# Hyena convolution in a diffusion backbone: spectra at odd half-bins, filters computed ahead of two norm gaps, u transformed from even and odd times apart

## The reference, cut to what matters

```python
def hyena_mixer(h, w_in, short_w, ..., bias, w_out):          # h: (1, 256, 1024)
    x0, x1, v = jnp.split(short_conv(h @ w_in, short_w), 3, axis=-1)
    h_fwd, h_bwd = hyena_filters(n, w1, b1, w2, b2, w3, b3, w4, freq)
    u = v * x1
    return (x0 * (bidirectional_long_conv(u, h_fwd, h_bwd) + u * bias)) @ w_out

def bidirectional_long_conv(u, h_fwd, h_bwd):                 # n = 256
    k = concatenate([h_fwd, zeros(1), h_bwd[1:][::-1]])       # 512 taps
    y = irfft(rfft(u, 512) * rfft(k, 512), 512)[:n]
```

## Time and profile before

| | |
|---|---|
| median of three runs | 1348.87 us |
| profiled execution, its own time | 1346.94 us |
| span of its trace | 1345.3 us |
| TensorE matmul busy | 1312.9 us, 98% |
| VectorE busy | 978.9 us, 73% |
| ScalarE busy | 633.8 us, 47% |
| POOL busy | 119.0 us, 9% |
| moved by DMA | 275.13 MB, mean 205 GB/s |
| mean granted TensorE clock | 0.999 |

### The profile page before, as it was taken

How to read it: one execution, slowest core, us unless ns; L and a number is a source line. 1 busy time by engine, 2 the same in 40 slices (tenths; PEclk the granted TensorE clock), 3 DMA queues, 4 the chain that set the end, 5 groups by cost and what they waited for, 6 DMA issues and landing times.

```text
span 1345.3 us, 21575 instructions
## 1 busy us (share of the span) xinstructions
PE 1312.9 (98%) x7850; PEld 1126.2 (84%) x7850; DVE 978.9 (73%) x1446; ACT 633.8 (47%) x969; POOL 119.0 (9%) x209
## 2 busy tenths in 40 slices
PE   5899999999999999999999999999999999999997
PEld 3678777887778988789999999999877888989996
DVE  5888777887776875668888578877765787865554
ACT  6633333323465575565444465444454434644443
POOL 3000010111000430011111001100000000000000
PEclk9999999999999999999999999999999999999999
DMA  9655666777656753269888649875533435656663
GB/s 357 215 173 189 215 215 223 239 256 263 214 159 190 190 155 89 94 214 353 309 301 287 184 156 328 310 220 178 161 116 110 138 112 192 237 183 184 184 184 105
DMA packets 76360, 275.13 MB, mean 205 GB/s; under 512 B 9226, under 2 KB 9781, under 8 KB 75712
## 3 DMA queue, kind: packets, MB, share of 16 engines
q1 hardware_dynamic: 52128, 187.00, 43.1%
q0 software_dynamic: 24160, 87.12, 19.3%
HBM read 273.04 MB, written 1.05 MB: 204 GB/s over the span
## 4 chain that ended last, share of the span: by engine, by line
PE 88%; DVE 5%; ACT 3%; DMA 2%; issue 1%; DVEq 0%; SPq 0%; ACTq 0%
PE gu L1670 17%; PE gu L1672 17%; PE gu L1671 17%; PE acc L1731 8%; PE acc L1733 8%; PE acc L1732 8%; PE acc L1720 1%; DMA wlo<-in_wstream_dram 1%; DVE wlo_r L1002 1%; PE acc L2140 1%; ACT whi L616 1%; PE acc L2016 1%; DVE wlo_r L1327 1%; PE acc L2027 1%; DMA x_lat<-in_x_in_dram 1%
## 5 line engine op out<-in xcount | busy, mean ns | idle before, releaser
L1670 PE MATMUL gu<-h_hi,whi 128*128 128x256 f32 (+1 forms) x1688 | 520.0, 308 | 3.6 <-DVE h_lo L1127 1.3
L1671 PE MATMUL gu<-h_lo,whi 128*128 128x256 f32 (+1 forms) x1688 | 514.6, 305 | 0.0
L1672 PE MATMUL gu<-h_hi,wlo_r 128*128 128x256 f32 (+1 forms) x1688 | 514.3, 305 | 0.0
L1002 DVE TENSOR_TENSOR wlo_r<-wlo,whi 128x1024 fp32r<-128x1024 f32 x350 | 421.6, 1222 | 95.9 <-ACT whi L616 94.2
L616 ACT ACTIVATE whi<-wlo 128x1024 fp32r<-128x1024 f32 x350 | 360.7, 1049 | 92.1 <-DMA wlo<-in_wstream_dram 91.6
L1670 PEld LDWEIGHTS gu<-h_hi,whi 128*128 128x128 f32 x1688 | 318.0, 188 | 31.9 <-issue 3.8
L1671 PEld LDWEIGHTS gu<-h_lo,whi 128*128 128x128 f32 x1688 | 318.1, 188 | 20.5 <-issue 2.1
L1672 PEld LDWEIGHTS gu<-h_hi,wlo_r 128*128 128x128 f32 x1688 | 318.6, 189 | 15.5
L1019 DVE SCALAR_TENSOR_TENSOR part<-wm,cvec,part 128x512 f32<-128x512 f32 x266 | 199.3, 749 | 6.8 <-DMA wm<-in_wmod_dram 0.2
L1731 PE MATMUL acc<-whi,act_hi 128*128 128x512 f32 x440 | 175.8, 400 | 1.7 <-DVE act_lo L1215 1.2
L1733 PE MATMUL acc<-wlo_r,act_hi 128*128 128x512 f32 x440 | 174.2, 396 | 0.0
(11 more groups left out here) (340 smaller groups left out, 1241.7 us busy)
## 6 DMA issues: line engine op xcount, KB each, us to landing
wlo<-in_wstream_dram SPq DMA_DIRECT2D x350, 512.0 KB, 3.7
wm<-in_wmod_dram POOLq DMA_DIRECT2D x132, 512.0 KB, 5.9
...
x_lat<-in_x_in_dram SPq DMA_DIRECT2D x1, 1024.0 KB, 7.8
area<-in_ctx_in_dram SPq DMA_DIRECT2D x1, 1024.0 KB, 8.8
```

The costliest lines, as they stand in the source:

```text
L1002: nc.vector.tensor_tensor(wlo[:, u.base % RING, :], raw[:, u.base % RING, :], whi[:, u.base % RING, :].bitcast(F32), ALU.subtract).then_in ...
L1670: nc.tensor.matmul(out_, w_hi, x_hi, start=start, stop=False, skip_group_check=True)
L1671: nc.tensor.matmul(out_, w_hi, x_lo, start=False, stop=False, skip_group_check=True)
L1672: return nc.tensor.matmul(out_, w_lo, x_hi, start=False, stop=stop, skip_group_check=True)
```

## The change

The transform's bins move from k to k + 1/2 (k = 0 to 255 of 512). No bin is then purely real, so the Nyquist spectra, their copies, the 1x512 product step and the zeroing of a row of `k_s` go: eight spectra in place of ten. The second block of 128 bins is stored in reverse order (255 down to 128), so that row k of it is bin 255-k.

Positions in time are stored even ones first, then odd ones: in the positional features, the window, the tables, and in u, whose transposes now take every second column (`th::2`). Between bins k and 255-k the cosine sums of the even times are equal and their sine sums have opposite signs; for the odd times it is the other way round. So `u_spectrum` makes one matmul per bank and not two (bank 0 even cosine, 1 odd sine, 2 odd cosine, 3 even sine), ScalarE copies banks 2 and 3 to SBUF (`odd_out`, one 1024-wide step for each half, ODD_AT), and VectorE adds them to and subtracts them from banks 0 and 1 (steps 0 and 1) into `u_f`, which lies in SBUF in the spare unit buffers. The four products then read `u_f` and no longer `acc`. A half has eight steps on VectorE, all 1024 wide.

The filters are computed in ffn(1), turns 8 to 10, with steps two units apart. Spectra 0 to 3 (first half of the channels) stand in the gap ahead of ffn(2), three ahead of the norm columns and one behind them, and the 16 warm-up matmuls of that gap are gone; spectra 4 to 7 stand in the same way in the gap ahead of the hyena stage. ScalarE copies two of each four between the steps of its norms and two behind `h_his` (`spectra_norms`). `filter_out(i)` waits only until VectorE has read the banks of the one before (FD_READ), not for its whole sums. The hyena units carry no spectra. The eight inverse transforms stay where they are.

The diff, cut to its core and less indented; new table values for the time order and half-bins stand at its end.

```diff
@@ -218,8 +218,8 @@
 def sem(name):
...
-spare_hi = sb("spare_hi", [P, UNIT], F32R)
-spare_lo = sb("spare_lo", [P, UNIT], F32R)
+spare, spare_r = both("spare", [P, 2, UNIT])
+spare_hi, spare_lo = spare_r[:, 0, :], spare_r[:, 1, :]
@@ -322,6 +321,7 @@
+u_f = spare[:, :, :].rearrange("p w (s n) -> p w s n", s=2)
@@ -388,7 +388,7 @@
 def spectrum_bank(i):
-    return [gu[:, 0, :], gu[:, 1, :], job_p[:, :]][i] if i < 3 else [mean_p[:, :], job_p[:, :]][(i - 3) % 2]
+    return four_banks[i % 4]
 def scores(i):
@@ -923,11 +924,6 @@
-    ffn(1, peeled=at_steps([(6, 2)], [lambda: batch_rows(1)]))
-    load_table(ACT.Sqrt)
-    norms(8, (U_FFN[2] + 2, U_FFN[2] + 3))
-    load_table(ACT.Silu)
     def sine(l):
@@ -937,24 +933,29 @@
-        if what == "nyquist":
-            ins = nc.scalar.activation(k_nyq[half][0:1, :], spectrum_bank(i)[0:1, :], ACT.Copy)
-        else:
-            ins = nc.scalar.activation((k_re if what == "re" else k_s)[:, w, cols], spectrum_bank(i), ACT.Copy)
-        ins.then_inc(fa, 1)
-    ffn(2, peeled=at_steps([ROWS_AT] + FILTER_AT, [lambda: batch_rows(2)] + [lambda l=l: sine(l) for l in range(3)]))
+        nc.scalar.activation((k_re if what == "re" else k_s)[:, w, cols], spectrum_bank(i), ACT.Copy).then_inc(fa, 1)
+    def spectra_norms(q, held, i):
+        square(q, 0)
+        square(q, 1)
+        split(Unit(held))
+        square(q + 1, 0)
+        spectrum_out(i)
+        square(q + 1, 1)
+        spectrum_out(i + 1)
+        split(Unit(held + 1))
+        h_his(q + 1)
+        spectrum_out(i + 2)
+        spectrum_out(i + 3)
+    ffn(1, peeled=at_steps([(6, 2)] + FILTER_AT, [lambda: batch_rows(1)] + [lambda l=l: sine(l) for l in range(3)]))
...
-    square(10, 0)
-    square(10, 1)
-    split(Unit(U_HY + 2))
-    spectrum_out(0)
-    square(11, 0)
-    square(11, 1)
-    spectrum_out(1)
-    split(Unit(U_HY + 3))
-    h_his(11)
-    spectrum_out(2)
+    spectra_norms(8, U_FFN[2] + 2, 0)
+    load_table(ACT.Silu)
+    ffn(2, peeled=at_steps([ROWS_AT], [lambda: batch_rows(2)]))
+    load_table(ACT.Sqrt)
+    spectra_norms(10, U_HY + 2, 4)
     def mixed_hi(c):
@@ -969,13 +970,16 @@
-        if idx < 7:
-            spectrum_out(3 + idx)
...
+        if idx in ODD_AT:
+            a.wait_ge(uf_done, 2 * ODD_AT[idx] + 1)
+            if ODD_AT[idx]:
+                a.wait_ge(yf_step, YF_STEPS)
+            nc.scalar.activation(product_b(0), acc[:, 2:4, :], ACT.Copy).then_inc(odd_out, 1)
@@ -1579,9 +1579,13 @@
-    ffn(2, peeled=at_steps([COEF_AT] + FILTER_AT, [lambda: (batch_out(2), norm_coef(13))]
+    ffn(1, peeled=at_steps([(7, 0)] + FILTER_AT, [lambda: (batch_out(1), norm_coef(9), norm_coef(11))]
...
+    norms(8, (U_FFN[2] + 2, U_FFN[2] + 3))
+    ffn(2, peeled=at_steps([COEF_AT], [lambda: (batch_out(2), norm_coef(13))]))
@@ -1620,28 +1624,25 @@
-        if step_ in (0, 2):
-            v.wait_ge(uf_done, 2 * g + step_ // 2 + 1)
-        if step_ == 4:
-            v.wait_ge(yf_step, YF_STEPS * g + 4)
-            nc.vector.tensor_tensor(product_b(1)[0:1, 0, :], acc[0:1, 2, :], k_nyq[g][0:1, :], ALU.mult).then_inc(yf_step, 1)
-            return
-        if step_ in (5, 6):
-            v.wait_ge(yf_step, YF_STEPS * g + (5 if step_ == 6 else 3))
-            dst = (re, s_)[step_ - 5]
-            nc.vector.tensor_tensor(dst, dst, product_b(step_ - 5), (ALU.subtract, ALU.add)[step_ - 5]).then_inc(yf_step, 1)
-            return
-        dst, banks, k_ = [(re, slice(0, 2), k_re), (s_, slice(0, 2), k_s),
-                          (product_b(0), slice(2, 4), k_s), (product_b(1), slice(2, 4), k_re)][step_]
-        nc.vector.tensor_tensor(dst, acc[:, banks, :], k_[:, :, cols], ALU.mult).then_inc(yf_step, 1)
+        if step_ < 2:
+            v.wait_ge(uf_done, 2 * g + 2)
+            v.wait_ge(odd_out, g + 1)
+            nc.vector.tensor_tensor(u_f[:, step_, :, :], acc[:, 0:2, :], product_b(0),
+                                    (ALU.add, ALU.subtract)[step_]).then_inc(yf_step, 1)
+        elif step_ < 6:
+            v.wait_ge(yf_step, YF_STEPS * g + 2)
+            dst, part_, k_ = [(re, 0, k_re), (s_, 0, k_s), (product_b(0), 1, k_s), (product_b(1), 1, k_re)][step_ - 2]
+            nc.vector.tensor_tensor(dst, u_f[:, :, part_, :], k_[:, :, cols], ALU.mult).then_inc(yf_step, 1)
+        else:
+            v.wait_ge(yf_step, YF_STEPS * g + step_ - 1)
+            dst = (re, s_)[step_ - 6]
+            nc.vector.tensor_tensor(dst, dst, product_b(step_ - 6), (ALU.subtract, ALU.add)[step_ - 6]).then_inc(yf_step, 1)
...
-        if idx == 10:
-            v.wait_ge(fa, 3 + 10)
-            step(nc.vector.memset(k_s[0:1, 0, :], 0.0))
-            settle()
+        if idx == min(YF_AT):
+            v.wait_ge(fa, 3 + len(SPECTRUM))
@@ -2064,17 +2065,13 @@
-    ffn(1, 4, peeled=at_steps([(6, 4)], [lambda: batch_columns(1)]))
-    norm_gap(9)
...
     def filter_layer(l):
...
-            pe.wait_ge(gate_free, 12)
+            pe.wait_ge(gate_free, 10)
@@ -2085,9 +2082,9 @@
-            pe.wait_ge(mod_ready, AHEAD + 3)
+            pe.wait_ge(mod_ready, AHEAD + 2)
...
-            pe.wait_ge(fd, FD_SUM[i - 1])
+            pe.wait_ge(fd, FD_READ[i - 1])
@@ -2096,50 +2093,58 @@
     def spectrum(i):
...
-        if i >= 4:
-            pe.wait_ge(fa, 3 + i - 1)
...
-            if what == "nyquist":
-                out_, w_, x_ = spectrum_bank(i)[0:1, :], dft[:, 2 + th, 0:1], p_f
-            else:
-                base = 0 if what == "re" else 2
-                out_, w_, x_ = spectrum_bank(i), dft[:, base + th, w * P:(w + 1) * P], p_f if what == "re" else m_f
-            ins = nc.tensor.matmul(out_, w_, x_[:, th, cols], start=(th == 0), stop=(th == 1))
+            base, x_ = (0, p_f) if what == "re" else (2, m_f)
+            ins = nc.tensor.matmul(spectrum_bank(i), dft[:, base + th, w * P:(w + 1) * P], x_[:, th, cols],
+                                   start=(th == 0), stop=(th == 1))
...
-    ffn(2, 5, peeled=at_steps([BATCH_AT] + FILTER_AT, [lambda: batch_columns(2)]
+    ffn(1, 4, peeled=at_steps([(6, 4)] + FILTER_AT, [lambda: batch_columns(1)]
...
+    pe.wait_ge(fd, FD_SUM[1])
+    spectrum(0)
+    spectrum(1)
...
-    for i in range(3):
+    spectrum(2)
+    norm_columns(9, 0)
+    norm_columns(9, 1)
+    spectrum(3)
+    pe.wait_ge(fa, 3 + 2)
+    ffn(2, 5, peeled=at_steps([(0, 5), BATCH_AT], [lambda: pe.wait_ge(fa, 3 + 4), lambda: batch_columns(2)]))
+    pe.wait_ge(mod_ready, AHEAD + 3)
+    pe.wait_ge(gate_free, 12)
+    for i in (4, 5, 6):
...
-    pe.wait_ge(fa, 3 + 2)
+    spectrum(7)
+    pe.wait_ge(fa, 3 + 6)
     def transposes(g):
...
-        pe.wait_ge(fa, 3 + 10)
+        pe.wait_ge(fa, 3 + len(SPECTRUM))
...
-                ins = nc.tensor.transpose(bank[:, c * P:(c + 1) * P], u_t[:, 4 * g + c, th * P:(th + 1) * P], ident[:, :])
+                ins = nc.tensor.transpose(bank[:, c * P:(c + 1) * P], u_t[:, 4 * g + c, th::2], ident[:, :])
...
     def u_spectrum(g, b):
-        if b == 0:
+        if b == 2:
...
-                pe.wait_ge(yf_step, 5)
-        base = 0 if b < 2 else 2
-        for th in range(2):
-            ins = nc.tensor.matmul(acc[:, b, :], dft[:, base + th, (b % 2) * P:(b % 2 + 1) * P],
-                                   u_n[:, th, g * 512:g * 512 + 512], start=(th == 0), stop=(th == 1))
-        if b % 2:
+                pe.wait_ge(yf_step, 2)
+        th, base = [(0, 0), (1, 2), (1, 0), (0, 2)][b]
+        ins = nc.tensor.matmul(acc[:, b, :], dft[:, base + th, 0:P], u_n[:, th, g * 512:g * 512 + 512],
+                               start=True, stop=True)
+        if b in (1, 3):
...
     def inverse(c):
@@ -2161,17 +2166,15 @@
-        if idx < 7:
-            spectrum(3 + idx)
...
-        if idx in UF_AT:
-            u_spectrum(*UF_AT[idx])
+        for g, b in UF_AT.get(idx, ()):
+            u_spectrum(g, b)
...
-        projected(Unit(U_HYO + c), c, c == 0, 8 + c + 1, (YF_STEPS + 2, YF_STEPS + 5) if c == 0 else None)
+        projected(Unit(U_HYO + c), c, c == 0, 8 + c + 1, (YF_STEPS + 2, YF_STEPS + 2) if c == 0 else None)
@@ -2205,13 +2208,13 @@
+FD_READ = [21 + 2, 26 + 2, 30 + 2, 35 + 2]
...
-SPECTRUM = [(half, what, w) for half in range(2) for what in ("re", "sine") for w in range(2)] \
-    + [(half, "nyquist", 0) for half in range(2)]
+SPECTRUM = [(half, what, w) for half in range(2) for what in ("re", "sine") for w in range(2)]
...
-FILTER_AT = [(6, 5), (7, 3), (8, 1), (8, 4), (9, 1), (9, 4), (10, 1)]
+FILTER_AT = [(8, 3), (8, 5), (9, 1), (9, 3), (9, 5), (10, 1), (10, 3)]
 def at_steps(places, calls):
@@ -2225,11 +2228,12 @@
-UF_AT = {11: (0, 0), 12: (0, 1), 13: (0, 2), 14: (0, 3), 18: (1, 0), 19: (1, 1), 20: (1, 2), 21: (1, 3)}
-YF_AT = {13: [(0, 0)], 14: [(0, 1)], 15: [(0, 2), (0, 3)], 16: [(0, 4), (0, 5), (0, 6)],
- 20: [(1, 0)], 21: [(1, 1), (1, 2), (1, 3), (1, 4)], 22: [(1, 5), (1, 6)]}
-YF_STEPS = 7
+ODD_AT = {12: 0, 18: 1}
+UF_AT = {11: [(0, 2), (0, 3)], 12: [(0, 0), (0, 1)], 18: [(1, 2), (1, 3), (1, 0), (1, 1)]}
```

(27 more changed lines are left out.)

## The result

The changed kernel takes 1339.5 us in the median of four runs (1335.43 to 1343.3), the kernel before in the same comparison 1349.36 us (1347.74 to 1352.38): ratio 0.9927, 95% interval 0.9907 to 0.9948. The forecast was 1334.2 us, in a range of 1329.6 to 1339.3. The direction was right; the gain is 9.9 us where 14.65 were forecast, and the time lies 0.2 us outside the range. Set beside the kernel before in a second comparison the changed kernel has 1340.1 us (ratio 0.9931, 0.9914 to 0.9947), so the miss of some 5 us is real.

The account below looks back on a forecast made before the run. TensorE was taken to bound the kernel (88% of the chain, busy 98% of the span). Terms -12.5 - 4.05 + 1.4 + 0 + 0.5 = -14.65 us took the median from 1348.87 to 1334.2 us, range 1329.6 to 1339.3.

Parts of the forecast that it names:

- A: Hyena units 0 to 11: with filter spectra 3 to 9 gone from behind units 0 to 6, 12.5 us less.
- B: Unit 11's end to the projection's end: u's 16 matmuls become 8, 6.9 us less work, 3.05 of stalls; -4.05 us.
- C: Gap ahead of ffn(2): three spectra replace the warm-up matmuls, a fourth follows the norm columns; +1.4 us, bounds +1.2 to +1.9.
- D: Gap ahead of the hyena: a spectrum added behind the norm columns costs 0, as TensorE still waits for VectorE's last h_lo.
- Rival 4: The two norm gaps do not hold four spectra each: C and D cost 4 us, not 1.4; 1336.8 us, chance 0.05.
- E: Filters moved from ffn(2) to ffn(1), steps two units apart: TensorE work unchanged, two waits for ScalarE's sine; +0.5 us.
- Less some 0.2 of drain each: In E's sine waits in ffn(1): some 0.2 us taken off each of two 0.45 us waits, giving +0.5.
- Rival 2: The forecast stalls do not come: B is -7.1 us and E 0, giving 1330.7 us; chance 0.17.
- rival 3: Hyena products behind units 13 to 22 cost far more, 2.1 us each cancelling the gain; slower than before, chance 0.02.
- Rival 1: VectorE sets the pace from hyena unit 13 on, so B brings nothing: 1338.3 us, chance 0.17.

## Why the prediction went wrong

*A* (-12.5 forecast, -12.45 measured) held, by the pitches of 2.84 us.

*B* (-4.05, measured -3.95) held. Its layout by hand put inverse(4) at 57.4 us behind unit 11's end, the taps of unit 19 at 34.0 and the end at 81.1; the trace has 57.30, 34.02 and 81.20, and VectorE's idle time ahead of those taps is 1.51. The account of it as work and stalls held less well: the stalls were laid out as 0.75, 0.85, 0.45 and 1.0 us, 3.05 in all, and TensorE's waits are 0.69 (unit 16), 0.70 (transposes), 0.16 (inverse(0)) and 0.73 (inverse(4)), 2.3 in all, yet the gain is no larger. What makes up the difference isn't shown by a run; likely it is the start behind each wait, since inverse(4) takes 1.99 us in the chain and the next inverse, which waits for nothing, 1.73. The strided transposes take 0.48 per four and not 0.44: 0.04, so the 0 that I took was nearly right. The Trainium skill's "SBUF — State Buffer", Door 1, had them free; the trace agrees to within 0.01 us per transpose. The products with both operands in SBUF take 1.218 and 1.220 us, those with a PSUM operand took 1.216 and 1.213:

```profile
L1635 DVE TENSOR_TENSOR area<-spare,area 128x1024 f32<-128x1024 f32 x4 | 4.9, 1218 | 0.0
...
L1635 DVE TENSOR_TENSOR wm<-spare,area 128x1024 f32<-128x1024 f32 x4 | 4.7, 1220 | 0.0
```

(groups by line; mean ns of one). The 62 cycles that the Trainium skill's "VectorE: DVE Perf Modes", TRN2 errata, has for the PSUM source don't show in steps of this shape; the measurement decides.

*C* (+1.4, measured +1.14, just under its own lower bound of +1.2) and *D* (0, measured 0) held. Rival 4 is refuted.

*E* failed, and alone accounts for the miss: +0.5 forecast, +5.67 measured. The step that failed is "Sine layer l+1 waits for ScalarE's sine, which ends 6.7 us after the end of the unit in front ... That occurs twice ... 2 x 0.45". Three things were wrong in it.
- The 6.7 us was read where the next step stood three or four units off, and used for steps two units apart. There it holds once (the wait of 0.44). The next sine is queued behind ScalarE's and VectorE's arrears from the one before, and comes 8.4 us after it: 1.90 us of wait. The waits sum to 2.34, not 0.9. Spread out, they go (the run with steps three units apart and the one with early layers, in which E would be 212.2 + 184.7 against 200.2 + 196.0, +0.8); put close together in the kernel before, they come, of the same size.
- I had no term for the clock. Of seven traces with an empty wait of 1.9 us there, five have the granted clock at 0.50 behind it (the changed kernel in three executions, the one with the buffer for odd bins, the kernel before with close steps) and two have not. With the wait filled (two traces) or gone (three) there is no fall. If the fall had nothing to do with the wait, all five of twelve would land on those seven by chance once in 38. Of the six in ffn(1), the stretch takes 216.6 to 217.3 us in the four with a fall and 213.5 and 213.9 us in the two without (u's matmuls twice, VectorE's sums twice): 3.3 us. In the kernel before with close steps the fall is shorter and costs 1.4. Here 2.34 + 3.3 = 5.6, all but 0.1 of the 5.67.
- "Less some 0.2 of drain each" took 0.4 off 0.9. In u's matmuls twice, where the clock did not fall, waits of 2.32 made the stretch 2.1 longer than it should be (213.5 against 200.2 + 11.3): 0.1 each.

The prediction named in advance what would show it: "if ffn(1) grows by over 2 us more than ffn(2) shrinks". It grew by 5.7 more. The range was drawn from the rivals of the hyena stage and the gaps; E, the cheapest term, had no upper end worth the name, and no rival.

Rival 2 (no stalls) is refuted by both places, and rival 3 by the 1.22 us of the products. Rival 1's time, 1338.3, is the nearest to the result, but not for its reason: VectorE does set the pace from unit 13's end to inverse(4), as its name says and as B's layout had it too, yet B brought what it was to bring. That the time fell near 1338.3 is chance.

What stays open: the clock's fall is tied to the wait by these twelve traces, but two in seven escaped it, and no run shows what decides that. No run varies the length of one wait with all else kept. The clock in the first 60 us differs from execution to execution: the gap ahead of ffn(1) is reached at 585.51 to 590.62 us in the kernels here. The one trace of the kernel before is the earliest, and the only one with 1.00 from 40 to 60 us. No run looks for the cause.
